# Four layers on one core: shape-ordered attention steps, masks in pairs, a late output row, pooling from the widest window, two squares summed on TensorE

## The reference, cut to what matters

```python
# indexer of the sparse mixer
logits = jnp.einsum('bqhd,bsd->bqhs', qib, k_idx)
score = jnp.einsum('bqhs,bqh->bqs', jax.nn.relu(logits), wb)
# each attention: masked scores, softmax, weighted values
s = jnp.where(mask, s, -jnp.inf); p = jax.nn.softmax(s, axis=-1)
# pooling, w in (2, 4, 8, 16), one window per group of 128 channels
pooled.append(mean_over_last_w_tokens - uf[:, :, g])
mixed = jnp.einsum('bsgd,gde->bsge', pooled, pool_w)
# last step of each half of the second pair of layers
x = x + rmsnorm(m, gain)
```

## Time and profile before

| what | value |
|---|---|
| median of three runs | 2418.17 us (2417.23 to 2418.5) |
| the profiled execution's own time | 2416.57 us |
| its span in the trace | 2414.8 us |
| mean granted TensorE clock | 0.997 |
| PE busy | 2371.4 us, 98% of the span |
| PE's waits in the list of waits | 31.6 us in all, the longest 8.2 us |

### The profile page before, as it was taken

One profiled execution on the slowest core, in us unless ns is written; L12 is line 12 of the kernel. 1 busy time (PEld: TensorE's weight loads), 2 busy tenths in 40 slices (PEclk: granted clock), 3 DMA queues, 4 the chain that ended last, 5 costly groups with the idle time before them and its releaser, 6 DMA issues. The chain is left out here.

```text
span 2414.8 us, 29460 instructions
## 1 busy us (share of the span) xinstructions
PE 2371.4 (98%) x11832; PEld 1900.5 (79%) x11832; DVE 1034.8 (43%) x1906; ACT 956.0 (40%) x1338; POOL 1049.1 (43%) x831
## 2 busy tenths in 40 slices
PE   8999999999999999999999999999999999999997
PEld 6777688888877767888888769888889779788887
DVE  4687531121348865221126445322225768322224
ACT  5345542232343455332235455422124485322223
POOL 4435244454444253444545453443444334444442
PEclk9999999999999999999999999999999999999999
DMA  5223122323222121323233212322332312322331
GB/s 167 76 62 106 36 96 96 105 88 105 83 93 88 53 97 53 105 88 105 89 104 101 87 36 71 105 84 90 105 98 95 105 53 88 105 90 85 105 105 53
DMA packets 139624, 214.40 MB, mean 89 GB/s; under 512 B 7776, under 2 KB 66272, under 8 KB 139232
## 3 DMA queue, kind: packets, MB, share of 16 engines
q1 hardware_dynamic: 139488, 212.51, 27.1%
HBM read 208.30 MB, written 2.10 MB: 87 GB/s over the span
## 5 line engine op out<-in xcount | busy, mean ns | idle before, releaser
L273 POOL TENSOR_TENSOR w_lo<-raw,w_hi 128x512 fp32r<-128x512 f32 (+1 forms) x776 | 992.3, 1313 | 1312.4 <-ACT w_hi L263 1312.1
L311 PE MATMUL ps<-h_hi,w_hi 128*128 128x512 f32 x1696 | 683.2, 403 | 11.3 <-POOL w_lo L273 11.1
L311 PE MATMUL ps<-h_hi,w_lo 128*128 128x512 f32 x1696 | 663.6, 391 | 0.0
L311 PE MATMUL ps<-h_lo,w_hi 128*128 128x512 f32 x1696 | 663.2, 391 | 0.0
L263 ACT ACTIVATE w_hi<-raw 128x2048 fp32r<-128x2048 f32 (+2 forms) x205 | 362.3, 1781 | 569.1 <-PE ps L311 443.8
L311 PE MATMUL ps<-hid_hi,w_hi 128*128 128x512 f32 x992 | 391.7, 395 | 4.7 <-DVE hid_lo L946 2.7
L311 PEld LDWEIGHTS ps<-h_hi,w_hi 128*128 128x128 f32 x1696 | 318.6, 188 | 92.7 <-issue 18.3
L311 PE MATMUL ps<-hid_hi,w_lo 128*128 128x512 f32 x992 | 387.2, 390 | 0.0
L311 PE MATMUL ps<-hid_lo,w_hi 128*128 128x512 f32 x992 | 387.0, 390 | 0.0
L311 PEld LDWEIGHTS ps<-h_lo,w_hi 128*128 128x128 f32 x1696 | 318.4, 188 | 70.1 <-issue 5.6
L311 PEld LDWEIGHTS ps<-h_hi,w_lo 128*128 128x128 f32 x1696 | 318.0, 187 | 70.5 <-issue 0.4
(11 more groups left out here) (302 smaller groups left out, 2800.8 us busy)
## 6 DMA issues: line engine op xcount, KB each, us to landing
raw<-in_w_up SPq DMA_DIRECT2D x32, 1024.0 KB, 5.3
raw<-in_w_down SPq DMA_DIRECT2D x32, 1024.0 KB, 5.0
raw<-in_ffn_w_gate SPq DMA_DIRECT2D x44, 512.0 KB, 4.0
raw<-in_ffn_w_up SPq DMA_DIRECT2D x44, 512.0 KB, 5.0
raw<-in_w_in SPq DMA_DIRECT2D x20, 1024.0 KB, 5.0
raw<-in_ffn_w_down SPq DMA_DIRECT2D x20, 1024.0 KB, 5.0
raw<-in_w_out SPq DMA_DIRECT2D x8, 1024.0 KB, 5.4
raw<-in_ev_w_in SPq DMA_DIRECT2D x8, 1024.0 KB, 5.3
```

The costliest lines, as they stand in the source:

```text
L273: pool.tensor_tensor(w_lo[slot.buf][:, k, 0:slot.width], raw[r][:, k, 0:slot.width], w_hi[slot.buf][:, k, 0:slot.width].bitcast(F32), ALU. ...
L311: mm = pe.matmul(o, lh, rh, start=first and q == 0, stop=last and q == 2, skip_group_check=True)
```

## The change

Six edits.

- `Attention.tensor`: the value products of units i-4 and i-3 now come at even steps, directly behind the scores; before, units i-5 and i-4 at odd steps. The steps that finish a head pair (output, high part, low part) move one step earlier, and each attention has one step less. Paces that hang on the number of steps follow.
- `Attention.vector`: at an even step DVE masks units i and i+1 one after the other and negates both maxima with one instruction; before, one mask and one negation a step.
- Indexer: four units at a time instead of two, and a group waits until all of the previous four banks are read.
- `out_c`: its tiles of row 3 for the first two output blocks come after the other six; the wait for row 3 (`mix_lo` 6) moves behind those six.
- Pooling: groups in the order 16, 8, 4, 2; the pooling matmuls at steps 17, 19, 20 and 22 (before 20 to 23); the output product's first group from step 24 in 8 steps (before 25 in 7), the second from step 32 in 6 steps (before 7).
- Last norm: the squares of the last two blocks are summed by matmuls of their own; DVE's addition of the third block goes. In the odd layer's first boundary the evacuation of bank 3 of the second half comes before the low parts of blocks 4 and 5.

```diff
@@ -22,6 +22,7 @@
+POOL_ORDER = (3, 2, 1, 0)
@@ -448,7 +449,7 @@
-                self.last_apart = False
+                self.apart = 0
@@ -472,14 +473,15 @@
-            if nm.last_apart:
-                pe.wait_ge(sems[nm.used], nm.used0 + nm.blocks - 2)
+            if nm.apart:
+                pe.wait_ge(sems[nm.used], nm.used0 + nm.blocks - 1 - nm.apart)
                 for i in range(2):
                     pe.matmul(ps[:, nm.bank, 0:S // 2], ones, two(nm.acc)[:, i, :], start=i == 0, stop=False)
-                pe.wait_ge(sems[nm.ready], nm.sq0 + nm.blocks)
-                to = nm.buf[(nm.blocks - 1) % 2]
-                for i in range(2):
-                    mm = pe.matmul(ps[:, nm.bank, 0:S // 2], ones, two(to)[:, i, :], start=False, stop=i == 1)
+                for k in range(nm.blocks - nm.apart, nm.blocks):
+                    pe.wait_ge(sems[nm.ready], nm.sq0 + k + 1)
+                    for i in range(2):
+                        mm = pe.matmul(ps[:, nm.bank, 0:S // 2], ones, two(nm.buf[k % 2])[:, i, :], start=False,
+                                       stop=k == nm.blocks - 1 and i == 1)
@@ -745,9 +747,12 @@
-                low(0, 2)
-                take(1, 3)
-                add_m(1, 2)
+                if self.split_first:
+                    low(0, 2)
+                    take(1, 3)
+                else:
+                    take(1, 3)
+                    low(0, 2)
@@ -755,6 +760,7 @@
+                add_m(1, 2)
@@ -812,7 +818,7 @@
-            SUMS, TURN_SUMS, OUT, HIGH, LOW = 2, 3, 5, 6, 7
+            SUMS, TURN_SUMS, OUT, HIGH, LOW = 2, 3, 4, 5, 6
@@ -882,15 +888,17 @@
-                return len(self.units) + self.VAL + 3
+                return len(self.units) + self.LOW
...
                         self.scores(pe, i)
-                    u = i - self.VAL - 1
+                    u = i - self.VAL
@@ -916,14 +924,15 @@
-                dve.wait_ge(*at("s_masked", self.u0 + i + 1))
-                sg["nmax"].by(dve.tensor_scalar(sn[:, i:i + 1], sx[:, i:i + 1], -SCALE, None, ALU.mult))
+                dve.wait_ge(*at("s_masked", self.u0 + i + 2))
+                sg["nmax"].by(dve.tensor_scalar(sn[:, i:i + 2], sx[:, i:i + 2], -SCALE, None, ALU.mult), 2)
...
                 for i in range(self.steps()):
-                    if i < n:
+                    if i < n and i % 2 == 0:
                         self.mask(dve, i)
+                        self.mask(dve, i + 1)
@@ -1093,7 +1102,7 @@
-            pl.n_out[1].last_apart = not even
+            pl.n_out[1].apart = 0 if even else 2
@@ -1189,8 +1198,8 @@
-            dil_pace = Pace(3 * 32, 0, dil.steps() - 3)
-            out_a, out_b0, out_b1 = Pace(16, 0, 3), Pace(8, 12, 6), Pace(8, 18, 5)
+            dil_pace = Pace(3 * 32, 0, dil.steps() - 2)
+            out_a, out_b0, out_b1 = Pace(16, 0, 3), Pace(8, 12, 6), Pace(8, 18, 4)
@@ -1270,26 +1279,26 @@
-                for i in range(0, len(units), 2):
+                for i in range(0, len(units), 4):
                     qb, h = units[i]
-                    idx_pace.emit(i, tiles)
-                    idx_pace.emit(i + 1, tiles)
+                    for u in range(i, i + 4):
+                        idx_pace.emit(u, tiles)
                     if i == 0:
...
                         pe.wait_ge(*at("kk_low", 1))
-                    if i == 2:
                         pe.wait_ge(*at("col_ready", 1))
                         pe.wait_ge(sems["ln_done"], pl.n_ckv.i + 1)
-                    if i >= 4:
-                        pe.wait_ge(*at("idx_relu", i - 2))
+                    else:
+                        pe.wait_ge(*at("idx_relu", i))
                     w, q = (qb + 1) * P, slice(qb * P, (qb + 1) * P)
-                    for n, (a_q, a_k) in enumerate(((q_hi, kk_hi), (q_hi, kk_lo), (q_lo, kk_hi))):
-                        for e in range(2):
-                            rows = slice(HD * e, HD * e + HD)
-                            mm = pe.matmul(ps[:, (i + e) % 4, 0:w], a_q[rows, h // 2, q], a_k[rows, 0:w],
-                                           start=n == 0, stop=n == 2)
-                            if n == 2:
-                                sg["idx_ready"].by(mm)
+                    for d in range(0, 4, 2):
+                        for n, (a_q, a_k) in enumerate(((q_hi, kk_hi), (q_hi, kk_lo), (q_lo, kk_hi))):
+                            for e in range(2):
+                                rows = slice(HD * e, HD * e + HD)
+                                mm = pe.matmul(ps[:, d + e, 0:w], a_q[rows, (h + d) // 2, q], a_k[rows, 0:w],
+                                               start=n == 0, stop=n == 2)
+                                if n == 2:
+                                    sg["idx_ready"].by(mm)
@@ -1350,9 +1359,9 @@
-                pe.wait_ge(*at("mix_lo", 6))
+                pe.wait_ge(*at("mix_lo", 5))
                 pe.wait_ge(*at("ret_lo", 2))
-                rest(tiles_of(pl.out_c, FEAT, hid_hi, hid_lo))
+                rest(group_tiles(pe, pl.out_c, FEAT, hid_hi, hid_lo, late=at("mix_lo", 6)))
@@ -1725,8 +1734,8 @@
-                PM = 20
-                out_a, out_b = Pace(16, 25, 7), Pace(16, 32, 7)
+                pool_steps = (17, 19, 20, 22)
+                out_a, out_b = Pace(16, 24, 8), Pace(16, 32, 6)
@@ -1768,8 +1777,9 @@
-                    for m, w in enumerate(POOL_W):
-                        pool.wait_ge(sems["bank_free"], BANKS + HALF * pl.pool + m + 1)
+                    for n, m in enumerate(POOL_ORDER):
+                        w = POOL_W[m]
+                        pool.wait_ge(sems["bank_free"], BANKS + HALF * pl.pool + n + 1)
@@ -1780,7 +1790,7 @@
-                        pool.wait_ge(*at("pool_in", m + 1))
+                        pool.wait_ge(*at("pool_in", n + 1))
@@ -1815,7 +1825,7 @@
-                    pool_tiles = tiles_of(pl.pool, FEAT)
+                    pool_tiles = tiles_of(pl.pool, [(n, m * P, P, None) for n, m in enumerate(POOL_ORDER)])
@@ -1828,10 +1838,11 @@
-                        g = i - PM
-                        if 0 <= g < 4:
+                        if i in pool_steps:
+                            g = pool_steps.index(i)
                             pe.wait_ge(*at("pool_in", g + 1))
-                            sg["pool_mm"].by(pe.matmul(ps[:, 4 + g, :], pw[:, g, :], u4[:, g, 16:], start=True,
+                            m = POOL_ORDER[g]
+                            sg["pool_mm"].by(pe.matmul(ps[:, 4 + g, :], pw[:, m, :], u4[:, m, 16:], start=True,
...
```

More of the change, by code:

```diff
@@ L1912, in pooling @@
                                 stream_hi(act, s0 + s + 1)
-                        g = i - PM
-                        if 0 <= g < 4:
+                        if i in pool_steps:
+                            g = pool_steps.index(i)
                             act.wait_ge(*at("pool_out", g + 1))
-                            sg["pool_hi"].by(act.activation(hid_hi[:, 4 + g, :], u4[:, g, 16:], ACT.Copy))
+                            m = POOL_ORDER[g]
+                            sg["pool_hi"].by(act.activation(hid_hi[:, 4 + m, :], u4[:, m, 16:], ACT.Copy))
                     fox.scalar(act, pooling)
@@ L2071, in pooling @@
                     def pooling(i):
-                        for m in range(4):
-                            if i == pool_pace.step_of(16 + 4 * (m + 1)) + 1:
-                                evac(dve, pl.pool, m, u4[:, m, 16:])
-                        g = i - PM
-                        if 1 <= g <= 4:
-                            dve.wait_ge(*at("pool_hi", g))
-                            sg["pool_lo"].by(dve.tensor_tensor(hid_lo[:, 3 + g, :], u4[:, g - 1, 16:],
-                                                               hid_hi[:, 3 + g, :].bitcast(F32), ALU.subtract))
-                        if 0 <= g < 4:
+                        for n, m in enumerate(POOL_ORDER):
+                            if i == pool_pace.step_of(16 + 4 * (n + 1)) + 1:
+                                evac(dve, pl.pool, n, u4[:, m, 16:])
+                        if i - 1 in pool_steps:
+                            g = pool_steps.index(i - 1) + 1
+                            dve.wait_ge(*at("pool_hi", g))
+                            m = POOL_ORDER[g - 1]
+                            sg["pool_lo"].by(dve.tensor_tensor(hid_lo[:, 4 + m, :], u4[:, m, 16:],
+                                                               hid_hi[:, 4 + m, :].bitcast(F32), ALU.subtract))
+                        if i in pool_steps:
+                            g = pool_steps.index(i)
                             dve.wait_ge(*at("pool_mm", g + 1))
-                            col = V_PSC + g
-                            sg["pool_out"].by(dve.tensor_scalar(u4[:, g, 16:], ps[:, 4 + g, :], vec[:, col:col + 1],
+                            m = POOL_ORDER[g]
+                            col = V_PSC + m
+                            sg["pool_out"].by(dve.tensor_scalar(u4[:, m, 16:], ps[:, 4 + g, :], vec[:, col:col + 1],
```

## The result

The kernel after takes 2433.84 us (median of 4 runs, 2432.02 to 2435.36) beside 2418.34 us for the kernel before on the same chip (2417.23 to 2418.84). The ratio is 1.0066, 95% interval 1.005 to 1.0082: 15.5 us slower, where the prediction said 9.7 faster. The profiled execution took 2435.36 us, its span is 2433.6.

What follows compares the result with a forecast made beforehand. PE, busy 98% of the span, was taken as the bound, through its own pace and waits. Terms 3.4 + 1.2 + 3.0 - 2.3 + 0 + 3.5 + 0.9 = 9.7 us gained gave 2408.5 us, range 2402.5 to 2417.

Steps and rivals of the forecast that it cites:

- the masks in pairs: Dilated attentions: with masks paired, turns wait less behind DVE's top-k round; 1.5 us a layer, 3.0 gained in all.
- Negations halved on DVE: Attentions: one joint negation for two units gains nothing, because the matmuls hide it; no loss was priced.
- its turn stands two steps on: Attentions: a pair's first exponential comes 0.6 to 0.8 us later, but tiles cover this before its turn; no cost.
- Rival (a): The low clock stays, as new waits replace the old in the pooling stretch; price 3.0 us, 2411.5 us, chance 14%.
- a sign against itself: The profile after: a 0.50 clock in a new place would make the prediction wrong; no size given.
- Shapes and the sparse attention: Attentions: 38 fewer array-shape changes on PE at 0.09 us gain 3.4; values ahead of retention's scores lose 2.3.
- The wait of the last values: End of the sparse attention: the last values wait for ACT's copy until 276.5, 2.2 us against 0.5 before.
- Late row: Output product after the sparse attention: removes the 1.36 us wait for row 3, already spent earlier; 0 in all.
- Indexer: Indexer in fours: 24 fewer shape changes gain 2.2 us, waiting for the fourth bank costs 0.5 a layer; net 1.2.
- Pooling: Widest group first: PE's 2.57 us wait for POOL and the 0.50 clock there go; 3.5 us gained.
- Last norm and boundary: Last norm: PE ends its sums earlier, 0.6 us; odd boundary: swapped evacuation closes a DVE hole, 0.3; together 0.9 gained.
- (c): Rival, slower: values behind the scores find ACT's copy late in every pair; 2426 us at 0.4 us each, chance 8%.

Runs made afterwards that it cites:

- a1: The kernel after with one mask and one negation a step, as before, all other edits kept; 2411.58 us, ratio 0.9973.
- f1: The kernel after with the joint negation over three columns, the third unused; 2434.23 us, ratio 1.0065.
- a3: The kernel after with both masks, then two single-column negations in place of the joint one; 2416.89 us, ratio 0.9996.
- a2: The kernel after with mask, negation, mask, negation at even steps, each negation single-column; 2410.58 us, ratio 0.9969.
- c3: The kernel before with only the pooling's order, steps and first output group changed; 2413.97 us, ratio 0.9984.
- c1: The kernel before with only the order of the attention steps changed, output product's second group in 6 steps; 2416.85 us, ratio 0.9997.
- e1: The kernel after with a single-column negation behind each mask and the sparse attention in the order of before; 2405.66 us, ratio 0.9948.
- f2: The kernel before with one unused 4-byte column that moves every buffer behind it in SBUF by 32 bytes; 2411.05 us, ratio 0.9968.
- d1: The kernel after with the joint negation as a tensor_tensor multiplication by a new column buffer, moving later buffers by 32 bytes; 2427.58 us, ratio 1.0038.

## Why the prediction was wrong

**The step that failed** is the one on the masks in pairs: +3.0 with bounds of 0 and 7.0, and the two sentences that went with it, "Negations halved on DVE: nothing, the matmuls hide it" and "its turn stands two steps on, covered by tiles". In its place the runs show -22.3 us (a1 to after): about +1.0 for the pairing (not clear of noise), -6.3 for the negations' place, -17.0 for the joint instruction. A loss was excluded without a reason from the rows, although the trace of before has no 128x2 negation; that is where an unknown operation was priced as if known. The same trace could have warned: its copy at 220.06 waited for POOL's instruction to end, as did 14 subtractions of L1670.

*The joint instruction.* I took two columns to cost what one does (0.15 us; free of POOL it is 0.17). But beside POOL it waits. The Trainium skill gives a reason, in SBUF — State Buffer (SBUF: two separate sides): VectorE and GpSimd share a port pair under an exclusive lock, which an instruction of VectorE in a two-port mode, or one with two SBUF inputs, cannot have while GpSimd's instruction holds it. The Trainium skill's page VectorE: DVE Perf Modes (What auto-detection actually checks) gives the two-port mode to one source and a destination in SBUF whose outermost non-unit sizes are both even or equal. The runs agree in three points: 128x2 tensor_scalar held (mean 361 ns), 128x2 tensor_tensor held (361), 128x3 held (347; equal sizes, which my expectation for f1 overlooked). On a single column that section says nothing; here it was never held (means of 152 to 154). That the lock is the mechanism was not tried by silencing POOL; it rests on the times at which the held instructions end (19 of 20 in the kernel after). A column count of 1 was an advantage of the kernel before that its trace showed and I did not read: POOL was busy 43%, and 46 single negations started beside it unharmed.

*Its place.* "Two steps on" is right for the turn's own exponential. But there is one bank for turning. A turn also needs ACT's copy of the unit before, and on ACT that copy stands behind the exponential of the new pair. So the pair's first exponential, 0.7 us later, delays the very next turn. a3 shows it with waits for the exponential (3.4 to 5.6 us against a2) and for the copy (1.8 to 4.8): 5.2 us more, while values and retention wait 2.3 us less. The two spans differ by 4.1 us, the medians by 6.3.

*The clock.* Rival (a) gave the low clock 3.0 us in one place. The pooling stretch was cured in after and c3, as forecast (in a1 0.50 stood there again, from about 1427 to 1430), and 0.50 came back at new places behind waits of 2.7 and 3.1 us, which the prediction named as a sign against itself.

**The other steps held in kind, and their sum in part by luck.** Without the masks the change gained 6.5 us for 6.7 forecast. Measured apart, order, indexer and pooling gave 1.5, 4.2 and 4.4 us, and last norm with boundary 0.2: 10.3 in all (9.3 by the stages). Terms that were too small and an overlap that was hardly counted made up for each other.
- Shapes and the sparse attention: 1.1 us forecast, 1.5 by the runs and 2.4 by the stages of c1. As foreseen, scores and values start 0.32 apart (144.17 to 144.49), and retention's outputs or scores wait in 4 places. The wait of the last values was put at 2.2 us near 276.5; in the kernel after it is 1.69 at 283.55.
- Late row: "0 in all, its time has been spent earlier" is what e1 shows from the other side. The gain of 1.65 a layer was there and the new order had spent it.
- Indexer: right in kind, too small (2.7 or more for 1.2); the price for the fourth bank was an estimate and nothing came of it.
- Pooling: 3.5 forecast, 4.0 to 4.4 measured in c3, clock 1.00. But it overlaps with the shapes of that attention, which the sum corrected by only 0.7.
- Last norm and boundary: 0.9 forecast (0.6 and 0.3), 0.2 measured: by the stages the boundary gained 0.4 and the last norm lost 0.2. The wait of the earlier trace rows fell from 1.72 to 1.03, but behind it stand eight instructions instead of four, and from the start of that wait to ACT's logarithm it took 3.79 us before (2400.49 to 2404.28) and takes 3.99 now (2419.08 to 2423.07):

```profile
2420.11 1.13 PE L479 MATMUL ps<-p_more,tab 128*128 128x256 f32 x4 [1.03 <-DVE acc L685]
2421.08 1.89 PE L483 MATMUL ps<-sq_both,tab 128*128 128x256 f32 x8
...
2423.07 0.47 ACT L500 ACTIVATE rs<-ps,singles 128x256 f32<-128x256 f32 x1 [0.83 <-PE ps L483]
```

I took the table's test at 2403.64 for the bound; PE's sums are.

**The rivals.** Slower did come, but not by (c). Values waited in 5 places, not in every pair, and c1, which has their new order and nothing else, is no slower than before. (c) had the right victim on the path, ACT's copy, and the wrong cause.

## What to carry to other kernels

Before two small instructions are joined into one, look at what else changes with the form: here two columns instead of one made a 0.15 us instruction take up to 1.24 us, waiting for another engine. Look for the wait in the trace at hand first: a group of one form whose instructions take either of two times, the longer ones inside another engine's instruction, shows it. Price every form that the trace has never shown with a loss as one bound. And for any instruction that starts later, follow the whole list of the engine that waits for it, since the one that hurts may be queued behind it for another reason.

## What the runs showed of the hardware

- An instruction of DVE can be held up to the end of POOL's running one. Held were negations of 2 and 3 columns (19 of 20 long ones in the kernel after end 0.02 to 0.03 us behind POOL's), copies of 512 columns (0.43 us alone, 0.87 to 1.30 held) and subtractions of two SBUF inputs (at most 0.70 alone, 1.61 to 1.63 held). Not held were negations of 1 column, reciprocals of 8, MAX8, MATCH_REPLACE8, and masks that read PSUM (692 ns at most in the kernel after, beside POOL and away from it). Those held to the end stood beside a TENSOR_TENSOR of POOL; beside a TENSOR_SCALAR of POOL one negation of 2 columns took 0.39 us and one copy of 512 (at 1426.13 in the kernel after) its usual 0.43.
- The address of the weights decides TensorE's pace. With weight buffers 2 and 3 of the last layers at 32 bytes past a multiple of 64, matmuls of 512 columns start 0.233 us apart (before, after), and 0.227 with them at a multiple of 64 (f2, d1); weights in buffers 0 and 1, which always lie at a multiple, have 0.227 throughout. f2 gains 7.1 us by that alone.
- In the kernel after, the waits of 2.7, 2.7 and 3.1 us on TensorE were each followed by 3 to 7 us at 0.50 of the clock, and one of 1.83 us (at 861.50) was not; in a1 one of 1.69 us (at 275.26) was. So the length of one wait does not decide it alone.
